# The start of a four-layer trunk: modulation in two halves of the features, the stream scaled in place, plain transposes, the context last

## The chip, the cores and the metric

The kernel is one program on one core of a Trainium2 chip. The metric is the device time in microseconds, the median of several runs. PE is TensorE, DVE VectorE, ACT ScalarE, POOL GpSimd and SP SyncE, which issues the DMAs.

## What is computed

Four layers (two HGRN2 recurrences, two short convolutions, each followed by a SwiGLU block) over a latent stream x of 1024 tokens by 1024 features and a context of 256 tokens, in fp32. The part at issue is the entry of the first layer:

```python
silu_c = jax.nn.silu(c)
silu_cc = jax.nn.silu(c_ctx)
...
mod = silu_c @ ada_w[l] + ada_b[l]
sh1, sc1, g1, sh2, sc2, g2 = [m[:, None, :] for m in jnp.split(mod, N_MOD, axis=-1)]
h = _modulate(_rmsnorm(x, norm_w[l, 0]), sh1, sc1)
...
hc = _modulate(_rmsnorm(ctx, norm_w[l, 0]), csh1, csc1)
```

`_rmsnorm` divides a row by its root mean square and multiplies by norm_w, `_modulate` is h * (1 + scale) + shift. h and hc are then multiplied by w_hgrn_in (1024 x 5120).

## The kernel before

All large products are made of three fp32r passes (`products`, L1396 to L1404): high part by high, low by high, high by low. The features lie on the partitions in the products, so x (tokens on partitions) is turned first. The weights come in panels of 128 output columns; the first two (forget gates of head 0) are split into high and low by GpSimd (`split_to`, L1204 and L1207), the third (`first_third`) by ScalarE and GpSimd.

Each engine has its own list of instructions, written by hand in the order in which they run; semaphores hold them together. What is done at the start:

- **SP** issues the small tables, then 16 blocks of ada_w in four groups of 2 MB (`ada_group`; groups 0 and 1 make the shift of features 0 to 511 and 512 to 1023, groups 2 and 3 the scale), panel 0, half of x, panel 1, the context, the other half of x.
- **Modulation.** Groups 0 and 2 are summed by VectorE (`start_acc`, 16 instructions each, L2809 and L2813; PE then adds over the partitions with ones, `start_sums`, L1541). Groups 1 and 3 are products of PE with the conditions padded to 128 columns (`start_products`, 8 products each, L1521); ScalarE copies the row out of PSUM (`ada_turn`) and PE turns it (`start_turn`, L1531). Then VectorE adds the bias and weighs (L2707, L2826) into `mods` and `in_scale`.
- **Norms.** ScalarE squares and sums a block of 128 tokens and takes the root (`x_norm`, `x_std`), VectorE the reciprocal, and a diagonal matrix of it (`diag_start`) is made. PE turns a square of x by multiplying with the diagonal (`turn`, L1436): transposed and scaled in one. In a later layer `turn` uses a plain transpose of rows scaled beforehand (L1435).
- **A turn** t covers two blocks of tokens and two of features, four squares. ScalarE modulates even t, VectorE odd t (`modulate`, L2840) into a ring of four tiles `mod_start`; ScalarE rounds to the high part (`h_hi`), VectorE subtracts for the low part (`low`, `h_lo`, L2707) and counts `h_ready`.
- **first_pair** on PE makes both gates' panels: for each half of the tokens and each of eight kb (a step of six products) it waits for `h_ready`, and the turns still to be made are put between the steps. The context's turns (t = 8 to 11) and its two blocks (`context_block`, 24 products of 256 columns each, both into one bank) stand between the two halves. The list goes on with the third panel (`first_third`), and from there on without turns.

An fp32 product (the modulation's, a diagonal's) is recorded as two matmul passes, so 8 products are x16 in the profile; a plain transpose is one.

## Time and profile before

| | |
|---|---|
| median of 3 runs | 2605.58 us (2605.37 to 2605.85) |
| profiled execution, span | 2600.0 us (no time of its own is listed beside the span) |
| PE busy | 2524.9 us, 97% |
| DVE busy | 1750.5 us, 67% |
| POOL busy | 1245.5 us, 48% |
| ACT busy | 1122.8 us, 43% |
| mean granted TensorE clock | 0.991 |
| DMA | 351.05 MB, mean 135 GB/s |

The span goes from the first to the last instruction; busy is the time in which an engine had an instruction, so that two engines' shares overlap. Idle time of an engine that nothing waits for costs nothing. The granted clock is 1 at 2.4 GHz and 0.5 at 1.2 GHz.

### The profile page before, as it was taken

What the parts mean: (1) busy time and instruction counts of PE and PEld (TensorE: products, weight loads), DVE (VectorE), ACT (ScalarE), POOL (GpSimd) and SP (SyncE); (2) the same over time, 40 slices, a digit from 0 to 9 for tenths busy, and PEclk for the clock granted to TensorE, in tenths of its full rate; (3) what the DMA queues carried; (4) which work ended last, traced back from release to release, by engine and by line L of the source; (5) the groups of instructions that cost most, each with busy time, mean ns of one, the idle gap of its engine ahead of it and who ended that gap; (6) DMA issues with size and microseconds to landing.
All of it is one profiled execution on the core that took longest, in us unless ns stands there. A gap on an engine that the chain in (4) does not pass through costs nothing.

```text
span 2600.0 us, 35820 instructions
## 1 busy us (share of the span) xinstructions
PE 2524.9 (97%) x12452; PEld 2115.7 (81%) x12452; DVE 1750.5 (67%) x2343; ACT 1122.8 (43%) x2124; POOL 1245.5 (48%) x811
## 2 busy tenths in 40 slices
PE   7999999999999989999999999999999999999998
PEld 5888888888878778888888877888787888888886
DVE  5377777767865566667667986666436555565888
ACT  5334534443443653343445475111264333434444
POOL 3121321432230037776768952444304776766983
PEclk8999999999999999999999999999999999999999
DMA  6223431441361343343456332333514323345533
GB/s 261 74 74 121 178 136 67 154 146 65 114 264 61 138 141 130 122 145 129 165 204 238 97 110 97 115 112 113 214 54 154 106 89 109 116 166 216 191 99 114
DMA packets 119634, 351.05 MB, mean 135 GB/s; under 512 B 12240, under 2 KB 12240, under 8 KB 116432
## 3 DMA queue, kind: packets, MB, share of 16 engines
q1 hardware_dynamic: 119504, 349.33, 38.1%
q8 instruction: 80, 1.31, 0.2%
q14 instruction: 50, 0.41, 0.0%
HBM read 258.58 MB, written 90.70 MB: 134 GB/s over the span
## 4 chain that ended last, share of the span: by engine, by line
PE 83%; DVE 7%; POOL 3%; ACT 3%; DMA 2%; issue 1%; SPq 1%; DVEq 0%; ACTq 0%; POOLq 0%
PE psum L1402 19%; PE psum L1403 19%; PE psum L1404 19%; PE psum L1975 4%; PE psum L1977 4%; PE psum L1976 4%; PE psum L1650 2%; PE psum L1652 2%; PE psum L1651 2%; PE psum L1602 2%; POOL row_unit_sum L1358 2%; PE psum L1616 1%; PE psum L1589 1%; PE psum L1572 1%; DVE k_all L2999 1%
## 5 line engine op out<-in xcount | busy, mean ns | idle before, releaser
L1402 PE MATMUL psum<-x_hi,unit 128*128 128x512 f32 x1232 | 481.5, 391 | 5.2 <-DVE x_lo L2707 5.2
L1403 PE MATMUL psum<-x_lo,unit 128*128 128x512 f32 x1232 | 480.0, 390 | 0.0
L1404 PE MATMUL psum<-x_hi,unit 128*128 128x512 f32 x1232 | 479.9, 390 | 0.0
L2707 DVE TENSOR_TENSOR c_set<-c_set,psum 128x512 f32<-128x512 f32 x352 | 233.8, 685 | 279.3 <-ACT c_set L2072 178.6
L1308 POOL TENSOR_TENSOR unit<-unit_sum,unit 128x512 fp32r<-128x512 f32 x200 | 294.4, 1480 | 5.8 <-ACT unit L2072 4.9
L1402 PEld LDWEIGHTS psum<-x_hi,unit 128*128 128x128 f32 x1232 | 231.9, 188 | 54.2 <-ACT c_set L2072 5.7
L1404 PEld LDWEIGHTS psum<-x_hi,unit 128*128 128x128 f32 x1232 | 231.7, 188 | 48.5
L1403 PEld LDWEIGHTS psum<-x_lo,unit 128*128 128x128 f32 x1232 | 231.9, 188 | 47.6
L1402 PE MATMUL psum<-h_hi,w_hi 128*128 128x512 f32 x624 | 262.6, 421 | 0.2 <-DVE h_lo L2707 0.2
L1975 PE MATMUL psum<-row_unit_hi,part_hi 128*128 128x512 f32 x616 | 241.8, 392 | 3.1 <-DVE part_lo L2707 1.8
L1404 PE MATMUL psum<-h_hi,w_lo 128*128 128x512 f32 x624 | 244.1, 391 | 0.0
L1403 PE MATMUL psum<-h_lo,w_hi 128*128 128x512 f32 x624 | 243.9, 391 | 0.0
L1977 PE MATMUL psum<-row_unit_hi,part_lo 128*128 128x512 f32 x616 | 240.5, 390 | 0.0
L1976 PE MATMUL psum<-row_unit_lo,part_hi 128*128 128x512 f32 x616 | 240.3, 390 | 0.0
L2707 DVE TENSOR_TENSOR part_lo<-part_raw,part_hi 128x512 fp32r<-128x512 f32 x154 | 186.1, 1211 | 64.0 <-ACT part_hi L2072 63.5
L2072 ACT ACTIVATE c_set<-psum 128x512 f32<-128x512 f32 x176 | 100.3, 597 | 265.3 <-PE psum L1404 265.3
L1302 POOL TENSOR_TENSOR unit_sum<-ffn_raw 128x512 f32<-128x512 f32 x80 | 108.6, 1357 | 197.2 <-PE psum L1402 197.2
L1302 POOL TENSOR_TENSOR unit_sum<-ffn_raw,ffn_raw 128x512 f32<-128x512 f32 x120 | 159.8, 1332 | 58.5 <-PE psum L1402 58.0
L1222 POOL TENSOR_TENSOR w_lo<-w_raw,w_hi 128x1024 fp32r<-128x1024 f32 x30 | 73.5, 2449 | 238.6 <-ACT w_hi L2072 238.6
L2072 ACT ACTIVATE unit<-unit_sum 128x512 fp32r<-128x512 f32 x200 | 126.0, 630 | 55.8 <-POOL unit_sum L1302 55.8
L1975 PEld LDWEIGHTS psum<-row_unit_hi,part_hi 128*128 128x128 f32 x616 | 116.1, 188 | 29.4 <-issue 3.4
L1402 PE MATMUL psum<-conv_h_hi,conv_w_hi 128*128 128x512 f32 x352 | 138.1, 392 | 0.4 <-POOL conv_w_lo L1207 0.4
(320 smaller groups left out, 5630.9 us busy)
## 6 DMA issues: line engine op xcount, KB each, us to landing
ffn_raw<-in_w_ffn_in SPq DMA_DIRECT2D x80, 512.0 KB, 5.1
part_raw<-parts_kept SPq DMA_DIRECT2D x154, 256.0 KB, 2.7
parts_kept<-part_sums SPq DMA_DIRECT2D x22, 1280.0 KB, 5.3
out_raw<-in_w_ffn_out SPq DMA_DIRECT2D x44, 512.0 KB, 7.4
w_raw<-in_w_hgrn_in SPq DMA_DIRECT2D x40, 512.0 KB, 3.6
ada_raw<-in_ada SPq DMA_DIRECT2D x32, 512.0 KB, 4.8
conv_ada_raw<-in_ada SPq DMA_DIRECT2D x32, 512.0 KB, 4.1
units_kept<-stage_unit SPq DMA_DIRECT2D x28, 512.0 KB, 2.9
```

What stands on the lines that cost most here:

```text
L1222: pool.tensor_tensor(place[1][:, :], w_raws[0][:, slot, :], place[0][:, :], ALU.subtract).then_inc(S["panel_split"], 1)
L1302: pool.tensor_tensor(units[(PRODUCTS * e + l) % 4][2][:, :], one, other, op).then_inc(S["unit_summed"], 1)
L1308: pool.tensor_tensor(unit[1][:, :], unit[2][:, :], unit[0][:, :], ALU.subtract).then_inc(S["unit_ready"], 1)
L1358: pool.tensor_tensor(row_unit(n)[2][:, :], one, other, op).then_inc(S["rows_summed"], 1)
L1402: begin = pe.matmul(out_ap, hi[:, a:b], rhs_hi, start=first, stop=False)
L1403: pe.matmul(out_ap, hi[:, a:b], rhs_lo, start=False, stop=False)
L1404: return begin, pe.matmul(out_ap, lo[:, a:b], rhs_hi, start=False, stop=last)
L1975: begin = pe.matmul(dst, of_hi[:, tokens], hi[:, :], start=g == 0, stop=False)
L1976: pe.matmul(dst, of_hi[:, tokens], lo[:, :], start=False, stop=False)
L1977: return begin, pe.matmul(dst, of_lo[:, tokens], hi[:, :], start=False, stop=g == FFN_GROUPS - 1)
L2072: nc.scalar.activation(dst, src, func, **kw).then_inc(S[sem], 1)
L2707: V.tensor_tensor(dst, a, b, op).then_inc(S[sem], 1)
```

## The change

SP loads panel 0 first, then groups 2 and 0 (scale and shift of features 0 to 511), the small tables, panel 1, half of x, groups 3 and 1, the rest of x, and the context at the end. The modulation is made in two halves. In each half the scale is 8 products of PE, and the shift is shared: VectorE sums the first half of its rows (8 instructions), PE multiplies the other (4 products), and PE adds both in one accumulation. VectorE copies three of the four rows out of PSUM. x and the context are scaled by VectorE in place (128 x 1024 for a block), `diag_start` is dropped, and `turn` becomes a plain transpose for this layer too. PE makes 22 idle products at the start instead of 12. The second half's modulation stands behind the first step of `first_pair`; the context's turns, norms and blocks come last. ScalarE loads the root's table ahead of the first block.

```diff
+START_ROWS = 2, 0, 3, 1
...
-SCALED = 2, 3
+SCALED = 0, 2, 3
...
-TURNS = ([(q, f) for f in range(4) for q in (0, 1)] + [(CTX_Q, f) for f in range(4)]
-         + [(q, f) for f in range(4) for q in (2, 3)],
+TURNS = ([(q, f) for f in range(4) for q in (0, 1)] + [(q, f) for f in range(4) for q in (2, 3)]
+         + [(CTX_Q, f) for f in range(4)],
          None,
...
-NORMED = ((0, 1, 2, 3, 8, 9, 4, 5, 6, 7), tuple(range(LAT)))
+NORMED = (tuple(range(LAT + CCH)), tuple(range(LAT)))
...
         def diag_of(inst, block):
-            i = normed(inst).index(block)
-            return diag_start[:, i % 6, :] if inst == 0 else diag[:, i % 4, :]
+            return diag[:, normed(inst).index(block) % 4, :]
 
         def scaled_of(inst, block):
 
+            if inst == 0:
+                return stream(0, block)
             return ys[0][block // 4][:, block % 4, :] if inst == 2 else x_scaled[block % 3][:, :]
...
-            small_load(cond_in[:, :], cond)
+            sp.dma_start(cond_in[:, :], cond).then_inc(S["cond_loaded"], 16)
...
+            panel(N_HEADS, 0, w_hgrn_in[0])
+            ada_group(START_ROWS[0])
+            ada_group(START_ROWS[1])
             small_load(bias[:, :], ada_bias)
             small_load(nw[:, :], norm_w)
             small_load(lbr[:, :], lb_raw)
             small_load(gn[:, :], gnorm)
             small_load(cw[:, :], conv_w)
...
-            for group in range(4):
-                ada_group(group)
-            panel(N_HEADS, 0, w_hgrn_in[0])
+            panel(N_HEADS + 1, 1, w_hgrn_in[1])
             x_load(x_start, 0)
             x_load(x_start, 1)
-            panel(N_HEADS + 1, 1, w_hgrn_in[1])
-            sp.dma_start(ctxt[:, :, :], ctx.rearrange("b p n -> p b n")).then_inc(S["ctx_loaded"], 16)
+            ada_group(START_ROWS[2])
+            ada_group(START_ROWS[3])
             x_load(x_start, 2)
             x_load(x_start, 3)
+            sp.dma_start(ctxt[:, :, :], ctx.rearrange("b p n -> p b n")).then_inc(S["ctx_loaded"], 16)
...
             def start_products(i):
 
-                g = 2 * i + 1
+                g = START_ROWS[i]
+                if i == 3:
+                    pe.wait_ge(S["ada_row_evac"], i)
                 pe.wait_ge(S[f"ada_first{g}"], 16)
-                for kb in range(KB):
+                first = 0 if g >= 2 else KB // 2
+                for kb in range(first, KB):
                     mm = pe.matmul(ada_row_out[i], cond_pad[:, kb, :],
                                    ada_first[:, ADA_GROUP * g + kb // 2, (kb % 2) * HALF:(kb % 2 + 1) * HALF],
-                                   start=(kb == 0), stop=(kb == KB - 1))
+                                   start=(kb == first), stop=(kb == KB - 1))
                 mm.then_inc(S["ada_row_full"], 1)
...
             def start_turn(i):
-                g = 2 * i + 1
+
+                g = START_ROWS[i]
                 pe.wait_ge(S["ada_row_evac"], i + 1)
+                if g < 2:
+                    pe.wait_ge(S["start_step"], KB * (g + 1))
                 for j in range(ADA_GROUP):
                     c = 2 * (ADA_GROUP * g + j)
-                    mm = pe.matmul(ada_first_out[:, c:c + 2], ada_turn[:, i, j * P:(j + 1) * P], ident[:, 0:2],
-                                   start=True, stop=True)
+                    mm = pe.matmul(ada_first_out[:, c:c + 2], ada_turn[:, i % 2, j * P:(j + 1) * P], ident[:, 0:2],
+                                   start=True, stop=g >= 2)
+                    if g < 2:
+                        for cond_of in range(2):
+                            mm = pe.matmul(ada_first_out[:, c + cond_of:c + cond_of + 1],
+                                           start_acc[:, g, cond_of, j * P:(j + 1) * P], ones[:, :],
+                                           start=False, stop=cond_of == 1)
                 return mm
...
-            for _ in range(12):
+            for _ in range(22):
                 pe.matmul(bank(2, 0, P), ident[:, :], ident[:, :], start=True, stop=True)
             pe.wait_ge(S["silu_done"], 2)
             start_products(0)
-            start_sums(0)
+            start_products(1)
             start_turn(0)
-            start_products(1)
-            start_sums(1)
             start_turn(1).then_inc(S["ada_first_done"], 1)
-            for t in range(5):
+            for t in range(4):
                 turn(0, t)
+            start_products(2)
...
+                    turns_at = {(0, 5): (8,), (0, 6): (9,), (0, 7): (10,), (1, 0): (11, 12), (1, 1): (13,), (1, 2): (14,),
+                                (1, 3): (15,), (1, 4): (16,), (1, 5): (17,), (1, 6): (18,), (1, 7): (19,)}
...
-                            pe.wait_ge(S["h_ready"], 12 * half + 2 * (kb // 2) + 2)
+                            pe.wait_ge(S["h_ready"], 8 * half + 2 * (kb // 2) + 2)
...
-                            if half == 0 and kb < 7:
-                                turn(0, 5 + kb)
-                            elif half == 1 and kb < 2:
-                                turn(0, 18 + kb)
-                        if half == 0:
-                            for t in range(12, 15):
+                            if (half, kb) == (0, 0):
+                                start_products(3)
+                                start_turn(2)
+                                start_turn(3).then_inc(S["ada_first_done"], 1)
+                                for t in range(4, 8):
+                                    turn(0, t)
+                            for t in turns_at.get((half, kb), ()):
                                 turn(0, t)
-                            pe.wait_ge(S["h_ready"], 12)
-                            context_block(0, 0)
-                            turn(0, 15)
-                            turn(0, 16)
-                            context_block(1, 1)
-                            turn(0, 17)
+                    pe.wait_ge(S["h_ready"], 20)
+                    context_block(0, 0)
+                    context_block(1, 1)
...
+            copy(junk_start[:, 0:1], eps[:, 0:1], "table_ready", ACT.Sqrt)
+            act.wait_ge(S["table_ready"], 1)
+
+            def x_norms(blocks):
+                for tb in blocks:
+                    if tb % 2 == 0:
+                        act.wait_ge(S[f"x_loaded{tb // 2}"], 16)
+                    x_norm(0, tb, junk_start)
+
+            x_norms(range(4))
+            act.wait_ge(S["cmod_done"], 3)
+            for t in range(4):
                 turned(0, t)
-            for tb in range(4, LAT):
-                if tb % 2 == 0:
-                    act.wait_ge(S[f"x_loaded{tb // 2}"], 16)
-                x_norm(0, tb, junk_start)
-            for t in range(8, 12):
+            act.wait_ge(S["ada_row_full"], 3)
+            copy(ada_turn[:, 0, :], ada_row_out[2], "ada_row_evac")
+            x_norms(range(4, LAT))
+            act.wait_ge(S["cmod_done"], 7)
+            for t in range(4, 8):
                 turned(0, t)
...
+                for t in range(8, 12):
+                    turned(0, t)
+                act.wait_ge(S["ctx_loaded"], 16)
+                for c in range(CCH):
+                    x_norm(0, LAT + c, junk_start)
                 gates_out(0)
                 for t in range(12, 16):
                     turned(0, t)
-                evacuate_ctx(0, z[FWD][:, 0:CTX])
-                for t in range(16, 18):
-                    turned(0, t)
-                evacuate_ctx(1, z[BWD][:, 0:CTX])
-                for t in range(18, 20):
+                act.wait_ge(S["panel_loaded0"], 32)
+                copy(first_third[0][:, :], w_raws[0][:, 0, :], "w_hi_done")
+                act.wait_ge(S["cmod_done"], 8)
+                for t in range(16, 20):
                     turned(0, t)
                 gates_out(1)
+                evacuate_ctx(0, z[FWD][:, 0:CTX])
+                evacuate_ctx(1, z[BWD][:, 0:CTX])
...
-                if inst in SCALED:
+                if inst in SCALED[1:]:
                     return
                 dve.wait_ge(S["x_rstd_done"], n + 1)
+                if inst == 0:
+                    V.tensor_scalar(stream(0, block), stream(0, block), x_rstd[:, c], None, ALU.mult
+                                    ).then_inc(S["diag_done"], 1)
+                    return
...
+            def start_sums(g):
+
+                dve.wait_ge(S[f"ada_first{g}"], 16)
+                for kb in range(KB // 2):
...
+            def start_row(i):
+
+                dve.wait_ge(S["ada_row_full"], i + 1)
+                if i >= 2:
+                    dve.wait_ge(S["ada_first_done"], 1)
+                V.tensor_copy(ada_turn[:, i % 2, :], ada_row_out[i]).then_inc(S["ada_row_evac"], 1)
...
+            dve.wait_ge(S["silu_done"], 1)
+            start_sums(0)
+            dve.wait_ge(S["small_loaded"], 16 * 5)
+            dve.wait_ge(S["params"], 1)
...
+            start_row(0)
             dve.wait_ge(S["consts"], 5)
-            for tb in range(4):
-                x_norm(0, tb)
-            dve.wait_ge(S["ada_first_done"], 1)
-            sums = ada_first_out.rearrange("p (m two) -> p two m", two=2)
-            tt(mods[:, 0:2 * KB], sums[:, 0, :], bias[:, 0:2 * KB], ALU.add, "cmod_done")
-            tt(cmods[:, :], sums[:, 1, :], bias[:, 0:2 * KB], ALU.add, "cmod_done")
-            dve.wait_ge(S["cmod_done"], 2)
-
-            def weigh(dst, scale, weights, sem):
-
-                V.scalar_tensor_tensor(dst, scale, 1.0, weights, ALU.add, ALU.mult).then_inc(S[sem], 1)
-
-            weigh(in_scale[:, 0:KB], mods[:, KB:2 * KB], nw[:, 0:KB], "cmod_done")
-            weigh(in_scale[:, 4 * KB:5 * KB], cmods[:, KB:2 * KB], nw[:, 0:KB], "cmod_done")
-            dve.wait_ge(S["cmod_done"], 4)
+            x_norm(0, 0)
+            start_row(1)
+            x_norm(0, 1)
+            start_mods(0)
+            x_norm(0, 2)
+            x_norm(0, 3)
...
+            for t in range(4):
+                start_turned(t)
+            low(0, 3)
+            start_sums(1)
+            x_norm(0, 4)
+            x_norm(0, 5)
+            start_row(3)
+            x_norm(0, 6)
+            start_mods(1)
+            modulate(5)
+            low(0, 4)
+            x_norm(0, 7)
+            low(0, 5)
+            for t in range(6, 20):
+                if t % 2 == 1:
+                    modulate(t)
+                if t == 12:
+                    x_norm(0, LAT)
+                    x_norm(0, LAT + 1)
+                if t > 6:
                     low(0, t - 1)
             low(0, 19)
```

### Order of the instructions at three places

Place 1: PE from its first product to the first product of the stream. Before:

```order
L1545 MATMUL psum<-ident 128x128 x12
L1521 MATMUL psum<-ada_first,cond_pad 128x512 x8
L1541 MATMUL psum<-ones,start_acc 128x1 x8
L1531 MATMUL psum<-ident,ada_turn 128x2 x4
L1521 MATMUL psum<-ada_first,cond_pad 128x512 x8
L1541 MATMUL psum<-ones,start_acc 128x1 x8
L1531 MATMUL psum<-ident,ada_turn 128x2 x4
L1436 MATMUL psum<-diag_start,x_start 128x128 x20
L1402 MATMUL psum<-h_hi,w_hi 128x512
```

And now (the rows of the second start turn stand shortened here, then the four turns, the third row's products, the first step's first product, and the fourth row's products behind that step):

```order
L1550 MATMUL psum<-ident 128x128 x22
L1527 MATMUL psum<-ada_first,cond_pad 128x512 x12
L1540 MATMUL psum<-ident,ada_turn 128x2 x5
L1544 MATMUL psum<-ones,start_acc 128x1 x2
...
L1438 MATMUL psum<-ident,x_start 128x128 x16
L1527 MATMUL psum<-ada_first,cond_pad 128x512 x8
L1405 MATMUL psum<-h_hi,w_hi 128x512
...
L1527 MATMUL psum<-ada_first,cond_pad 128x512 x4
```

All modulation stood ahead of the first turn; now half of it stands behind turns 0 to 3, eight of its products directly ahead of the stream's first product.

Place 2: VectorE from the parameters of the forget gates (`lb_exp`, `lb`, `q_scale`) and the sums to its first reciprocals. Before, the parameters stood ahead of all sums:

```order
L2722 RECIPROCAL lb_exp<-lb_exp 128x8
L2707 TENSOR_TENSOR lb_exp<-lb_exp 128x8
L2707 TENSOR_TENSOR lb<-lb_exp 128x8
L2728 TENSOR_SCALAR one_minus_lb<-lb 128x8
L2730 TENSOR_SCALAR q_scale<-one_minus_lb 128x8
L2809 TENSOR_SCALAR start_acc<-ada_first,silu_cond 128x512 x2
L2813 SCALAR_TENSOR_TENSOR start_acc<-ada_first,silu_cond,start_acc 128x512 x14
```

And now, from the first sums to the second row copy:

```order
L2789 SCALAR_TENSOR_TENSOR start_acc<-ada_first,silu_cond,start_acc 128x512 x6
L2700 TENSOR_TENSOR lb_exp<-lbr,lb_exp 128x8
L2829 RECIPROCAL lb_exp<-lb_exp 128x8
L2700 TENSOR_TENSOR lb_exp<-lb_exp 128x8
L2700 TENSOR_TENSOR lb<-lb_exp 128x8
L2835 TENSOR_SCALAR one_minus_lb<-lb 128x8
L2837 TENSOR_SCALAR q_scale<-one_minus_lb 128x8
L2797 COPY ada_turn<-psum 128x512
L2713 RECIPROCAL x_rstd<-x_std 128x1
L2718 TENSOR_SCALAR x_start<-x_start,x_rstd 128x1024
L2797 COPY ada_turn<-psum 128x512
```

The parameter instructions, two row copies and the first scaling have come between the sums and PE's second start turn, which waits for the second row copy.

Place 3: VectorE in the second half of the tokens, around the context's scaling (the first h_lo is the low of turn 10, the second that of turn 11). Now:

```order
L2857 TENSOR_SCALAR mod_start<-psum,in_scale,mods 128x256 x2
L2700 TENSOR_TENSOR h_lo<-mod_start,h_hi 128x2x256
L2713 RECIPROCAL x_rstd<-x_std 128x1
L2718 TENSOR_SCALAR ctxt<-ctxt,x_rstd 128x1024
L2713 RECIPROCAL x_rstd<-x_std 128x1
L2718 TENSOR_SCALAR ctxt<-ctxt,x_rstd 128x1024
L2700 TENSOR_TENSOR h_lo<-mod_start,h_hi 128x2x256
```

Before, four diagonals for blocks 4 to 7 stood at the like place, ahead of the lows of the context's last two turns:

```order
L2840 TENSOR_SCALAR mod_start<-psum,in_scale,cmods 128x256 x2
L2738 RECIPROCAL x_rstd<-x_std 128x1
L2750 TENSOR_SCALAR diag_start<-ident,x_rstd 128x128
...
L2707 TENSOR_TENSOR hc_lo<-mod_start,hc_hi 128x512 x2
```

The low of turn 11, for which the third step of the second half waits, now stands behind both scalings of the context.

## Rows read from the trace of the kernel before

**Rows 1.** Busy time by stretch: us; busy (instructions) of each engine; granted clock; DMA; GB/s
```profile
45.22:91.07 45.85, 42.29 (x264) 37.16 (x265) 27.15 (x51) 27.05 (x53) 2.61 (x1) 1.00 0.13 39
68.30:71.28 2.98, 2.98 (x24) 2.98 (x25) 2.15 (x4) 1.98 (x4) 0.00 (x0) 1.00 0.60 176
91.07:130.00 38.93, 38.93 (x188) 32.87 (x187) 5.17 (x8) 14.17 (x18) 7.18 (x3) 1.00 0.27 94
```

**Rows 2.** Timeline of PE: start us, duration us, engine, line, operation, count
```profile
16.85 8.49 PE L1521 MATMUL psum<-ada_first,cond_pad 128*128 128x512 f32 x16 [9.80 <-DMA ada_first<-in_ada]
...
27.77 7.11 PE L1521 MATMUL psum<-ada_first,cond_pad 128*128 128x512 f32 x16
34.73 1.84 PE L1541 MATMUL psum<-ones,start_acc 128*128 128x1 f32 x16
...
46.68 1.05 PE L1436 MATMUL psum<-diag_start,x_start 128*128 128x128 f32 x8
47.49 0.48 PE L1402 MATMUL psum<-h_hi,w_hi 128*128 128x512 f32 x1
...
91.07 0.39 PE L1402 MATMUL psum<-h_hi,first_third_hi 128*128 128x512 f32 x1
```

**Rows 3.** Chain of waits, start of the program: start us, us, what
```profile
36.01 1.05 ACT junk_start L2072 x2
...
45.22 0.47 PE psum L1402
```

**Rows 4.** Timeline of SP's queue, DMA issues (columns as in rows 2)
```profile
1.27 0.42 SPq L804 DMA_DIRECT2D bias<-in_ada_bias  x1
...
3.63 4.95 SPq L834 DMA_DIRECT2D ada_first<-in_ada  x4
```

**Rows 5.** Timeline of VectorE
```profile
7.91 0.17 DVE L2730 TENSOR_SCALAR q_scale<-one_minus_lb 128x8 f32<-128x8 f32 x1
11.69 0.88 DVE L2809 TENSOR_SCALAR start_acc<-ada_first,silu_cond 128x512 f32<-128x512 f32 x2 [3.61 <-DMA ada_first<-in_ada]
12.49 9.36 DVE L2813 SCALAR_TENSOR_TENSOR start_acc<-ada_first,silu_cond,start_acc 128x512 f32<-128x512 f32 x14
...
39.33 1.17 DVE L2826 SCALAR_TENSOR_TENSOR in_scale<-mods,nw 128x8 f32<-128x8 f32 x1
...
49.54 0.69 DVE L2707 TENSOR_TENSOR h_lo<-mod_start,h_hi 128x512 fp32r<-128x512 f32 x1 [0.18 <-ACT h_hi L2072]
...
64.81 3.44 DVE L2707 TENSOR_TENSOR hc_lo<-mod_start,hc_hi 128x512 fp32r<-128x512 f32 x2
...
128.64 0.83 DVE L3053 TENSOR_SCALAR gates_f<-gates_f 128x1280 f32<-128x1280 f32 x1
```

**Rows 6.** Timeline of GpSimd
```profile
28.31 5.45 POOL L1204 TENSOR_TENSOR w_hi<-w_raw,zero 128x1024 fp32r<-128x1024 f32 x1 [19.12 <-DMA w_raw<-in_w_hgrn_in]
...
36.16 1.88 POOL L1204 TENSOR_TENSOR w_hi<-w_raw,zero 128x1024 fp32r<-128x1024 f32 x1
38.12 2.35 POOL L1207 TENSOR_TENSOR w_lo<-w_raw,w_hi 128x1024 fp32r<-128x1024 f32 x1
65.09 2.61 POOL L1222 TENSOR_TENSOR first_third_lo<-w_raw,first_third_hi 128x1024 fp32r<-128x1024 f32 x1 [24.62 <-ACT first_third_hi L2072]
```

**Rows 7.** Busy time by stretch, PE alone: us, PE busy, granted clock
```profile
7.05:9.42 2.37, 0.00 (x0) 1.00 1.00 410
9.42:19.66 10.24, 2.81 (x4) 0.50 1.02 414
40.14:43.54 3.40, 3.40 (x19) 0.50 1.02 405
```

**Rows 8.** Timeline of PE, plain transposes in a later stage
```profile
1879.73 0.60 PE L1435 MATMUL psum<-ident,x_scaled 128*128 128x128 f32 x4
1880.08 0.48 PE L1650 MATMUL psum<-conv_row,mixed_hi 128*128 128x512 f32 x1
```

**Rows 9.** Timeline of ScalarE
```profile
74.03 0.36 ACT L2072 ACTIVATE z_f<-psum 128x256 f32<-128x256 f32 x1
```

128 lines of the change are left out of this document (47 added, 81 removed).

## The prediction

> **What bounds the kernel now.** Read the busy time by stretch first [rows 1]: from 91.07 to 130 us PE is busy without a gap, and between 45.22 and 91.07 us it is idle for 3.6 of 45.85 us. At 91.07 us stands the third panel's first product [rows 2]; from there on the program is the same in both kernels, so what moves this start moves the end by as much, and I carry the rest over unchanged. The chain of waits [rows 3] names the first GEMM product at 45.22 us as the end of the start-up. The sum is made against the span of the profiled execution, 2600.0 us; the median of the runs, 2605.58 us, is 5.6 us above it and I add the difference in time to the median. A measurement of this kernel can tell about 0.2%, 5.2 us, from no change.
>
> **When the data land.** The first large transfer was issued at 3.63 us and its 2 MB were used at 11.69 us; the next group at 16.85 us, so a group takes 5.16 us and the rest, 2.9 us, is latency [rows 2, 4, 5]. After the change the first weight panel (0.5 MB, 1.3 us) goes out at 1.27 us, the second issue's slot, so it lands at about 5.4, ada group 2 at 10.6, group 0 at 15.8. Then the small tables and panel 1 (about 18), the stream's first two parts (20.5 and 23), groups 3 and 1 (28 and 33), the rest by 41 us. None of the later ones is waited for.
>
> **The new front half.** VectorE's sums over group 0 are now 8 instructions: 0.8 us for the first two, 6 x 0.67 us from 9.36 us / 14 [rows 5], 4.8 us in all, from 15.8 to 20.6. PE's 8 products on group 2 cost 7.1 us at full clock (the second x16 of [rows 2]) and end at about 17.7, the 4 on group 0 end at 21.3. They are not on the path of VectorE. On VectorE stand next the five parameter instructions (0.2 us each [rows 5], and a wait for ScalarE's exponential: 1.2 us), a row copy from PSUM (0.6), a block's scaling in place, another row copy (0.6). The scaling in place is 128x1024 and not in the trace; below it stands the 128x1280 tensor_scalar at 0.83 us, so 0.7 us, plus 0.2 for the reciprocal: 0.9 (bounds 0.8 and 1.4). Sum: 20.6 + 3.3 = 23.9 us.
>
> To this comes **GpSimd**. It splits panel 1 with two instructions of 1.88 and 2.35 us, and panel 1 now lands during VectorE's sums. In the trace such an instruction and VectorE's never ran at the same time: GpSimd's first took 5.45 us while the sums ran, against 1.88 alone [rows 6], and VectorE's 128x8 weighing took 1.17 us and its pair of lows 3.44 us instead of 1.3 while GpSimd was in one [rows 5]. At the first gap, behind the first parameter instruction, GpSimd gets in, and again behind the third. I take the full 1.88 + 2.35 = 4.2 us (bounds 0 and 4.2), so the second row copy ends at 28.1 us.
>
> The Trainium skill, SBUF — State Buffer, section SBUF: two separate sides, says that the pair of ports goes to whichever of the two engines starts first, for the whole instruction. The rows agree on the blocking, but not on who is next: GpSimd waited through five of VectorE's instructions from 28.31 us on, and through one behind 64.81 us [rows 5, 6]. By the page alone my sum, 2609.0 us, stands; the first of these two rows makes room for the second rival.
>
> Then PE turns the second row and adds the sums: 4 + 8 small products, 24 passes at 1.84/16 = 0.115 us, 2.7 us: 30.8. Modulation of the first half 0.7, two more blocks scaled 1.8: 33.3. Turns 1 to 3 at 0.4 us: 34.5. Here PE meets start_products(2), 8 products, 7.1 us: 41.6. First GEMM step 1.4 us (six products; 1.46 from 45.22 to 46.68 with the start of the first [rows 2, 3]): 43.0. **So the first GEMM product comes at about 41.6 instead of 45.2, but alone.** Behind it stand 4 more products (3.6), the two turns (0.9 and 2.7): 50.2. And PE is idle from 21.3 to about 26.5, so its clock falls: in the trace idling from 7.1 us brought the granted clock to half (1.2 GHz) at 9.42 us, where it stayed until 19.66, after 2.8 us of dense products; and the small products from 34.7 us on, with turns and a pause behind them, brought it down again at 40.14 for 3.4 us [rows 2, 7]. I charge one such stretch at half speed under the products, 3.4 / 2 = 1.7 us (bounds 0 and 6). The last start turn ends at **51.9 us**.
>
> **From there to the third panel.** PE has 16 turns, 15 GEMM steps and the two context blocks. A turn by a diagonal took 0.81 us from 46.68 to 47.49 [rows 2], and about 0.08 more in the product behind it; four plain transposes of the same size took 0.35 from 1879.73 to 1880.08 [rows 8], so 0.44 with the same extra. 16 x 0.44 + 15 x 1.38 + 5.9 (two context blocks, 2.98 us each [rows 1]) = 33.7 us. The saving of transposes, 20 x 0.45 = 9 us, is what the change truly removes; the 8 added products (7.1 us) give most of it back. Four waits remain. From a turn's end to the product that uses it I count 2.85 us for modulate, high and low: the turn whose last pass went out by 47.49 [rows 2] had its second low done at 50.23 [rows 5], and 0.1 for the handover.
> - Turn 9 stands in front of only one GEMM step and a turn: 2.85 - 1.8 = 1.0 us.
> - Turn 11 stands behind the first step of half 1. ScalarE does its high part and then the context's two norms (2 x 1.37 us: 1.05 for the squares [rows 3], the rest the root and handovers), and VectorE's low of turn 11 stands behind both scalings of the context (the third place of the order shown above). So 2.0 + 2.7 + 0.9 + 0.8 = 6.4 us after the turn, with 2.2 us of cover: 4.2 us.
> - Turn 19 is the last thing before context_block(0, 0), with no cover: 2.85 us.
> - Both context blocks use one bank; the copy of 0.36 us [rows 9] and its two handovers: 0.8 us.
>
> Together 8.9 us, where before it lost 3.6 [rows 1]. 51.9 + 33.7 + 8.9 = **94.5 us** against 91.07: 3.4 us later, 2609.0 us.
>
> **Costed at nothing:** the 22 idle products (they end near 9.1 us, before the data at 10.6; without them the products on group 2 would start at half clock and end some 1.5 us later, while the second row's copy waits for VectorE until 27.5 in any case); ScalarE's early table load (at about 21 us, ahead of the second block); the small tables behind group 0 (the parameters wait for group 0 anyway); the dropped diagonals; ScalarE's copy of the third panel's first part, now behind turned(15) (needed some 15 us later). The modulation's shift by PE and VectorE together saves VectorE 16 instructions of 0.67 us; the half of it that goes from the path is in the 4.8 us above.
>
> **The rivals.**
> 1. *PE at half clock longer* (slower). The small start products at 27 to 31 us and at 47 to 51 us keep PE sparse, as those at 34.7 us did. If the clock is at 1.2 GHz in start_turn(1), in all of the first 7 us of products and again in the first GEMM steps, that adds 2 + 1.7 + 1.7: 96 to 100 us, 2611 to 2615 us. For: the pause on PE ahead of them, over 5 us, is longer than the 2.4 us after which the clock fell the first time, and the second fall came with PE three quarters busy. Against: it was back 2.8 us after dense products began at 16.85 us. It decides when the products of start_products(2) still run at half after the first 3 us.
> 2. *GpSimd is kept out* until VectorE waits for PE at 28 us: the 4.2 us fall away, 2604.8 us. For: five instructions passed it at 28.31 us. Against: the parameter chain has gaps, and GpSimd's pass of 65.09 us was let in behind the one VectorE instruction that was running.
> 3. *The front half pays off* (faster): no collision, clock kept, and the context's norms finding ScalarE early, so that the 4.2 us wait halves: 94.5 - 4.2 - 1.7 - 2.1 = 86.5, 2601.0 us, and a little less in each price gives over 0.2%. For: PE has 9 us less of transposes. Against: it needs all three.
> 4. *It does not do what it says:* the first product no earlier than 45 us, as start_products(2) stands ahead of it. That is a half of rival 1, not a case of its own.
>
> **Chances.** Forecast 0.38, rival 1 0.34, rival 2 0.16, rival 3 0.12. The forecast and rival 2 lie within 0.2% (0.54); rival 1 is slower (0.34), rival 3 faster (0.12). The range reaches from the middle of rival 3 to the end of rival 1, 2601 to 2615 us.
>
> **What would show it.** First GEMM product near 42 to 45 us; a pause of 4 us on PE in half 1 before its third step, ended by VectorE; another near 3 us before the context products; GpSimd's w_hi of panel 1 longer than 4 us, or parameter instructions of VectorE of 2 us; granted clock 0.5 between 24 and 35 us; third panel at 94 us. I would be wrong if PE passes from the start turns to 90 us with under 5 us idle, or if anything behind the third panel has moved.

## The result, and the profile after

The changed kernel took 2613.49 us (median of 5 runs, 2612.66 to 2615.98), the kernel before 2605.37 us (5 runs, 2604.80 to 2605.85). The ratio is 1.0036, 95% interval 1.0025 to 1.0048: 8.1 us slower, more than the 0.2% that a measurement can tell from no change. The forecast was 2609.0 us, and its likeliest case "within 0.2%"; what came lies in rival 1's 2611 to 2615 us, and so inside the range.

Busy time by stretch of the changed kernel, from the first GEMM product to the third panel (columns as in rows 1), and behind it the three stretches at half clock up to there (columns as in rows 7):

```profile
47.68:101.99 54.31, 46.65 (x250) 38.53 (x249) 29.62 (x58) 29.80 (x57) 2.40 (x1) 0.94 0.09 28
```

PE alone:

```profile
25.60:42.70 17.10, 13.65 (x52) 0.50 1.03 409
56.40:59.80 3.40, 3.40 (x18) 0.51 0.00 0
80.20:83.70 3.50, 3.50 (x11) 0.51 0.00 0
```

Against [rows 1] the stretch grew from 45.85 to 54.31 us: PE is idle there for 7.66 us instead of 3.56, and busy for 4.36 us more although it turns by plain transposes; but the stretch now also holds the fourth row's products and two start turns (7.3 us, from 49.47 to 56.73), and the clock is 0.94 instead of 1. Ahead of it, half speed lasts from 25.6 to 42.7 us, where before it fell mostly into an idle wait for data [rows 7]. The timeline of PE (columns as in rows 2):

```profile
26.30 1.87 PE L1540 MATMUL psum<-ident,ada_turn 128*128 128x2 f32 x8 [5.19 <-DVE ada_turn L2797]
29.33 0.58 PE L1540 MATMUL psum<-ident,ada_turn 128*128 128x2 f32 x2 [1.17 <-DVE ada_turn L2797]
...
34.47 1.09 PE L1438 MATMUL psum<-ident,x_start 128*128 128x128 f32 x4
37.15 2.80 PE L1438 MATMUL psum<-ident,x_start 128*128 128x128 f32 x12 [1.58 <-DVE x_start L2718]
39.74 8.51 PE L1527 MATMUL psum<-ada_first,cond_pad 128*128 128x512 f32 x16
47.68 0.79 PE L1405 MATMUL psum<-h_hi,w_hi 128*128 128x512 f32 x1
...
56.73 3.42 PE L1438 MATMUL psum<-ident,x_start 128*128 128x128 f32 x16
59.90 0.48 PE L1405 MATMUL psum<-h_hi,w_hi 128*128 128x512 f32 x1
...
71.80 0.50 PE L1405 MATMUL psum<-h_hi,w_hi 128*128 128x512 f32 x1 [0.73 <-DVE h_lo L2700]
...
80.04 0.64 PE L1405 MATMUL psum<-h_hi,w_hi 128*128 128x512 f32 x1 [3.89 <-DVE h_lo L2700]
...
95.42 0.39 PE L1405 MATMUL psum<-hc_hi,w_hi 128*128 128x256 f32 x1 [2.56 <-DVE hc_lo L2700]
...
99.03 0.38 PE L1405 MATMUL psum<-hc_hi,w_hi 128*128 128x256 f32 x1 [0.47 <-ACT z_f L2076]
...
101.99 0.40 PE L1405 MATMUL psum<-h_hi,first_third_hi 128*128 128x512 f32 x1
```

The first GEMM product stands at 47.68 us, 2.5 us later than before [rows 2]; I had expected it 3.6 us earlier. The third panel stands at 101.99 us instead of 91.07, 10.9 us later. start_turn(1) goes from 29.33 to 34.47 us: 5.1 us for 24 passes, 0.21 us for each where [rows 2] show 0.115. The four waits of the second part (0.73, 3.89, 2.56, 0.47 us) are 7.65 us.

What PE waited for until 26.30 and 29.33 us are two row copies of VectorE, and these stand behind its sums. Three of the six longer sums, from windows of VectorE's timeline that hold one each:

```profile
17.83 0.75 DVE L2789 SCALAR_TENSOR_TENSOR start_acc<-ada_first,silu_cond,start_acc 128x512 f32<-128x512 f32 x1
18.49 2.38 DVE L2789 SCALAR_TENSOR_TENSOR start_acc<-ada_first,silu_cond,start_acc 128x512 f32<-128x512 f32 x1
20.80 2.82 DVE L2789 SCALAR_TENSOR_TENSOR start_acc<-ada_first,silu_cond,start_acc 128x512 f32<-128x512 f32 x1
```

What follows them on VectorE:

```profile
24.64 0.20 DVE L2829 RECIPROCAL lb_exp<-lb_exp 128x8 f32<-128x8 f32 x1 [0.27 <-ACT lb_exp L2076]
...
25.56 0.68 DVE L2797 COPY ada_turn<-psum 128x512 f32<-128x512 f32 x1
27.73 0.16 DVE L2713 RECIPROCAL x_rstd<-x_std 128x1 f32<-128x1 f32 x1 [1.49 <-ACT x_std L2076]
27.93 0.75 DVE L2718 TENSOR_SCALAR x_start<-x_start,x_rstd 128x1024 f32<-128x1024 f32 x1
28.59 0.68 DVE L2797 COPY ada_turn<-psum 128x512 f32<-128x512 f32 x1
```

And in the timeline of its ScalarE:

```profile
24.39 0.21 ACT L2076 ACTIVATE lb_exp<-lb_exp 128x8 f32<-128x8 f32 x1 [6.19 <-DVE lb_exp L2700]
24.62 1.28 ACT L2076 ACT_TABLE_LOAD   x1
...
26.15 1.06 ACT L2076 ACTIVATE junk_start<-x_start 128x1024 f32<-128x1024 f32 x1
```

The 8 sums of VectorE end at 24.2 us, not 20.6. The third of the six took 0.75 us, the fourth 2.38 and the fifth 2.82, and beside these two stand the two passes of GpSimd over panel 1:

```profile
17.98 2.35 POOL L1207 TENSOR_TENSOR w_hi<-w_raw,zero 128x1024 fp32r<-128x1024 f32 x1 [4.57 <-DMA w_raw<-in_w_hgrn_in]
20.41 2.67 POOL L1210 TENSOR_TENSOR w_lo<-w_raw,w_hi 128x1024 fp32r<-128x1024 f32 x1
```

The high pass ended at 20.33 us and the fourth sum 0.55 us behind it; the low pass ended at 23.08 and the fifth sum again 0.55 us behind it. So each pass held up one sum, and both together cost 3.7 us (7.78 us for the six sums, where e2 below has 4.06).

Then ScalarE: it sat 6.19 us in front of the exponential that waits for VectorE's parameter, loaded the root's table, and only at 26.15 us began the norm of a block that had been there since about 20.5 us. So VectorE waited 1.49 us, and the second row copy stands behind that wait.

### The profile page after: what moved, and what is told of

Its sections match the earlier page's. It is cut to its first block, busy times and chain, and to the rows that moved or that the text cites. A ratio compares the mean times of both kernels' runs of the same rounds, so it can differ in the third digit from the quotient of the medians.

```text
span 2613.1 us, 35752 instructions
## 1 busy us (share of the span) xinstructions
PE 2537.0 (97%) x12424; PEld 2121.4 (81%) x12424; DVE 1748.5 (67%) x2338; ACT 1121.3 (43%) x2120; POOL 1242.3 (48%) x811
## 4 chain that ended last, share of the span: by engine, by line
PE 85%; DVE 6%; POOL 3%; ACT 2%; issue 2%; DMA 2%; SPq 0%; DVEq 0%; ACTq 0%; POOLq 0%
PE psum L1405 19%; PE psum L1407 19%; PE psum L1406 19%; PE psum L1979 4%; PE psum L1981 4%; PE psum L1980 4%; PE psum L1654 2%; PE psum L1656 2%; PE psum L1655 2%; PE psum L1606 2%; POOL row_unit_sum L1361 2%; PE psum L1620 1%; PE psum L1593 1%; PE psum L1576 1%; PE psum L1438 1%
## 5 line engine op out<-in xcount | busy, mean ns | idle before, releaser
L1979 PEld LDWEIGHTS psum<-row_unit_hi,part_hi 128*128 128x128 f32 x616 | 115.6, 188 | 29.3 <-issue 3.4
L1407 PEld LDWEIGHTS psum<-h_hi,w_lo 128*128 128x128 f32 x624 | 117.4, 188 | 25.7
```

Source lines behind the costliest of these rows:

```text
L1407: return begin, pe.matmul(out_ap, lo[:, a:b], rhs_hi, start=False, stop=last)
L1979: begin = pe.matmul(dst, of_hi[:, tokens], hi[:, :], start=g == 0, stop=False)
```

## The experiments

Twelve kernels were run, four or two at a time on one chip together with the kernel before. The medians of before in these sets were 2603.39 to 2604.37 us, with single runs from 2601.7 to 2609.0, so single edits are told apart better by where the third panel starts in the trace than by the time. Each position is read from the one profiled execution of its kernel. Half clock is the sum of the stretches at 0.5 up to the third panel.

| kernel | ratio to before, 95% | third panel, us | first GEMM product | half clock, us |
|---|---|---|---|---|
| before | | 91.07 | 45.22 | 13.7 |
| changed | 1.0036 (1.0025 to 1.0048) | 101.99 | 47.68 | 23.9 |
| e1, PE kept busy | 1.0033 (1.0022 to 1.0044) | 99.96 | 45.59 | 13.7 |
| e2, split of panel 1 late | 1.0022 (1.0012 to 1.0031) | 98.20 | 43.84 | 20.5 |
| e3, tables first | 1.0028 (1.0019 to 1.0037) | 102.24 | 44.92 | 27.3 |
| e4, context late | 1.0019 (1.0010 to 1.0028) | 98.04 | 47.73 | 20.5 |
| e5, row copies together | 1.0036 (1.0024 to 1.0048) | 100.40 | 46.08 | 23.9 |
| e6, before with plain transposes | 1.0010 (1.0001 to 1.0019) | 93.49 | 47.86 | 27.3 |
| e7, four edits | 0.9999 (0.9990 to 1.0009) | 93.16 | 39.75 | 20.5 |
| e8, 12 idle products | 1.0046 (1.0033 to 1.0060) | 102.37 | 46.43 | 30.7 |
| e9, e7 with turns early | 0.9981 (0.9972 to 0.9990) | 87.20 | 40.18 | 17.1 |
| e10, e9 with dense passes | 0.9981 (0.9972 to 0.9990) | 87.17 | 40.61 | 13.7 |
| e11, e9 filled | 0.9978 (0.9969 to 0.9987) | 88.29 | 40.36 | 13.7 |
| e12, e11 and start_turn(3) | 0.9988 (0.9979 to 0.9997) | 91.52 | 42.10 | 17.1 |

What lies behind the third panel is not quite the same in each execution: span less third panel was 2508.9 us before, 2511.1 in the changed kernel, and 2507.9 to 2511.5 in the others. The clock is a part of it, not all: of this rest 36.1 us were at half clock before and 43.2 us in the changed kernel, but 40.0 us in e1, which has the longest rest, and 31.9 us in e12, whose rest is 2510.4 us.

### e1: is it the pauses that cost the clock?

```diff
             start_products(1)
+            idle_products(20)
             start_turn(0)
+            idle_products(4)
             start_turn(1).then_inc(S["ada_first_done"], 1)
-            for t in range(4):
+            turn(0, 0)
+            idle_products(9)
+            for t in range(1, 4):
                 turn(0, t)
```

> Edit: idle products on PE (20 ahead of start_turn(0), 4 ahead of start_turn(1), 9 between the first and the second turn), so that PE is not idle while it waits for VectorE. Clock theory: in the changed kernel start_turn(1) took 5.1 us where full clock gives 2.7, turns 1 to 3 took 2.6 instead of 1.2 and start_products(2) 8.5 instead of 7.1; with PE kept busy the granted clock stays at 1 from 21 to 48 us, the first GEMM product comes at about 44 us instead of 48.1, turns 4 to 7 take 1.8 us, and the third panel starts near 96.5 us instead of 102.2: 5 to 6 us faster, about 2608 us. Rival, the chain of VectorE and GpSimd: turns 1 to 3 wait for the scalings of blocks 2 and 3 anyway, so at most 2.4 us of the 5 come through, about 2611 us. If the idle products push out the products on which the program waits, no gain at all.

Measured: third panel 2.0 us earlier, and no difference in time that can be shown. From 10.6 us up to the first GEMM product PE had no pause over 1 us, and the clock fell all the same, 5.1 us later than in the changed kernel, inside start_turn(1). Busy time by stretch of e1, PE alone:

```profile
30.70:37.50 6.80, 6.80 (x34) 0.50 1.03 410
```

PE's timeline in e1, and VectorE's:

```profile
34.23 3.74 PE L1534 MATMUL psum<-ident 128*128 128x128 f32 x18
37.81 1.47 PE L1438 MATMUL psum<-ident,x_start 128*128 128x128 f32 x12
```

```profile
35.12 0.75 DVE L2726 TENSOR_SCALAR x_start<-x_start,x_rstd 128x1024 f32<-128x1024 f32 x1
```

Ten us less at half clock gave 2.0 us. That is the rival's size, but not by its cause alone. Up to 29.3 us PE waits for VectorE in both kernels, so that the clock gives nothing there. Behind it the steps got 3.9 us shorter: start_turn(1) 1.1 us (3.98 instead of 5.14), turns 1 to 3 1.3 us, start_products(2) 1.5 us. About 1.8 us of this went to the nine idle products, which ran at half clock themselves and took 3.7 us: VectorE's scaling of block 3 ended at 35.87 us, and turn 1 had to wait behind them until 37.81.

### e2: GpSimd out of the sums

```diff
-            for slot in range(2):
-                split_to(N_HEADS + slot, slot, ring[slot])
+            split_to(N_HEADS, 0, ring[0])
+            pool.wait_ge(S["ada_row_evac"], 2)
+            split_to(N_HEADS + 1, 1, ring[1])
```

> Edit: GpSimd starts splitting panel 1 only when both row copies of VectorE are done (ada_row_evac at 2). Collision theory: VectorE's sums then end at about 21 us instead of 24.2 (its hole of 2.6 us from 20.95 on goes) and the split, 4.2 us, falls into 28 to 33 us, where VectorE waits for PE; the second row copy ends 1.5 to 3.5 us earlier, and the third panel with it: about 2611 us. Rival: ScalarE's norm of block 0 (exponential behind VectorE, table load, x) is the later one, so that the row copy gains nothing and the split now meets the modulation instead: no change or 1 us slower.

The third panel came 3.8 us earlier, a little more than the theory had for the row copy (1.5 to 3.5); 0.25 us of it is an earlier landing of group 0. VectorE's six last sums took 4.06 us where they had taken 7.78, and GpSimd met a scaling of VectorE that nothing waited for (2.42 us instead of 0.75). VectorE's timeline in e2:

```profile
16.26 4.06 DVE L2790 SCALAR_TENSOR_TENSOR start_acc<-ada_first,silu_cond,start_acc 128x512 f32<-128x512 f32 x6
...
25.43 2.42 DVE L2719 TENSOR_SCALAR x_start<-x_start,x_rstd 128x1024 f32<-128x1024 f32 x1
```

So the collision costs 3.7 us, all of it on the path. The rival falls: ScalarE's norm moved forward as well, since its exponential had waited for the same sums.

### e3: the small tables and the parameters first

```diff
             panel(N_HEADS, 0, w_hgrn_in[0])
+            small_load(bias[:, :], ada_bias)
...
+            small_load(cw[:, :], conv_w)
             ada_group(START_ROWS[0])
             ada_group(START_ROWS[1])
-            small_load(bias[:, :], ada_bias)
...
```

On VectorE the parameter block moves ahead of start_sums(0).

> Edit: SP issues the five small tables ahead of both modulation groups, and VectorE does its six parameter instructions before the sums instead of behind them. ScalarE then has its exponential and the root's table before x lands. Theory: the row copy follows the sums at once (1.3 us earlier) and x_norm(0, 0) starts at 20.5 us when x lands instead of 26.2; the second row copy ends about 2.5 us earlier, at 26.8 instead of 29.3 us. Third panel 2 to 3 us earlier, about 2611 us. Rival: group 0 lands later by what the small tables take of the DMA engines, up to 2 us, which gives most of it back: same within 1 us.

Group 0 landed 1.7 us later (first sum at 17.37 instead of 15.71), and the second row copy still ended 1.3 us earlier; with a shorter half clock in front (13.7 us instead of 17.1) the first GEMM product came 2.8 us earlier. But the third panel stood at 102.24: behind that product the clock was low for 13.7 us (53.0 to 59.9, 80.3 to 83.7 and 94.0 to 97.4 us) instead of 6.9. The rival's result, and its cause took a part only: the later landing cost about half of the gain at the row copy, the clock the rest.

### e4: the context out of the way of turn 11

```diff
-                act.wait_ge(S["ctx_loaded"], 16)
-                for c in range(CCH):
-                    x_norm(0, LAT + c, junk_start)
                 gates_out(0)
-                for t in range(12, 16):
+                for t in range(12, 14):
+                    turned(0, t)
+                act.wait_ge(S["ctx_loaded"], 16)
+                for c in range(CCH):
+                    x_norm(0, LAT + c, junk_start)
+                for t in range(14, 16):
                     turned(0, t)
```

VectorE does x_norm(0, LAT) and x_norm(0, LAT + 1) behind low(0, 13) instead of ahead of low(0, 11).

> Edit: ScalarE does the context's two norms behind turned(13) instead of ahead of turned(12), and VectorE scales the context behind low(13) instead of ahead of low(11). Theory: the pause of 3.9 us ahead of the third step of half 1 falls to under 1 us (turn 11 to product is 2.85 us, cover 2.2), and the stretch at half clock behind it (1.7 us) goes too: 3 to 5 us faster, 2608.5 to 2610.5 us. Rival: the same wait turns up later, ahead of the fifth or seventh step (turns 13 to 15) or of the context's turns, since ScalarE has the same 2.7 us of norms and 1.2 us of gates to do: under 1 us faster.

Third panel 4.0 us earlier. The wait of 3.89 us is 0.30, a new one of 0.78 stands ahead of the context's first turn, and the half clock from 80.2 us on is gone. PE's timeline in e4:

```profile
76.52 0.50 PE L1405 MATMUL psum<-h_hi,w_hi 128*128 128x512 f32 x1 [0.30 <-DVE h_lo L2702]
...
82.63 0.63 PE L1438 MATMUL psum<-ident,ctxt 128*128 128x128 f32 x4 [0.78 <-DVE ctxt L2720]
```

### e5: both row copies together

```diff
             start_row(0)
+            start_row(1)
             dve.wait_ge(S["consts"], 5)
             x_norm(0, 0)
-            start_row(1)
             x_norm(0, 1)
```

> Edit: VectorE makes both row copies one behind the other and only then scales blocks 0 and 1. In the changed kernel the second row copy stood behind x_norm(0, 0), which waited 1.5 us for ScalarE's root at 27.6. Theory (the start hangs on the chain of VectorE up to start_turn(1)): the second copy ends at about 26.9 instead of 29.3 us, the modulation and the third panel come about 2.4 us earlier, about 2611 us. Rival (data and ScalarE's norms bound the turns as well): the scalings of blocks 2 and 3 stand in front of turns 1 to 3 in either order, so that under 1 us comes through.

1.6 us came through of the expected 2.4 (third panel 100.40), because start_turn(0), 1.9 us at half clock, now stands in the path ahead of start_turn(1). The clock stretches are as in the changed kernel, 23.9 us.

### e6: one part of the change alone, on the kernel before

```diff
-SCALED = 2, 3
+SCALED = 0, 2, 3
...
+                if inst == 0:
+                    V.tensor_scalar(stream(0, block), stream(0, block), x_rstd[:, c], None, ALU.mult
+                                    ).then_inc(S["diag_done"], 1)
+                    return
```

ScalarE's four diagonals are dropped; loads, sums and order stay.

> The kernel before with one part of the change alone: x and the context are scaled in place by VectorE and turned by plain transposes, ScalarE's four diagonals fall away; loads, modulation and order stay. Theory: the 20 turns cost 0.44 instead of 0.89 us each. 5 of them stand before the first GEMM product (45.22 us) and gain 2 us at most; 15 stand between it and 91.07, where PE was idle for 3.6 us only: 6 to 7 us less work, of which a part turns into waits for modulate, high and low (2.85 us each, as in the changed kernel). Third panel at 84 to 88 us, that is 3 to 7 us faster than before. Rival: the chain of modulate, high and low on VectorE and ScalarE, and VectorE's scalings of 0.75 us in place of the 128x128 diagonals, bound these steps already, so that the time is the same within 1.5 us.

Neither: the third panel came 2.4 us **later**, the time is 1.0010 of before. The first GEMM product is 2.6 us later, and from it to the third panel it takes 45.63 us, as before (45.85). The saving of 0.45 us for each turn is there and is lost to waits. PE's timeline in e6:

```profile
47.86 0.47 PE L1404 MATMUL psum<-h_hi,w_hi 128*128 128x512 f32 x1 [1.37 <-DVE h_lo L2705]
...
66.45 0.89 PE L1437 MATMUL psum<-ident,x_start 128*128 128x128 f32 x4 [2.56 <-DVE x_start L2741]
70.26 1.94 PE L1437 MATMUL psum<-ident,x_start 128*128 128x128 f32 x8 [2.91 <-DVE x_start L2741]
...
78.22 0.39 PE L1404 MATMUL psum<-hc_hi,w_hi 128*128 128x256 f32 x1 [1.67 <-ACT z_f L2074]
```

VectorE's timeline in e6:

```profile
34.05 2.87 DVE L2741 TENSOR_SCALAR x_start<-x_start,x_rstd 128x1024 f32<-128x1024 f32 x1
...
66.46 2.84 DVE L2741 TENSOR_SCALAR x_start<-x_start,x_rstd 128x1024 f32<-128x1024 f32 x1
```

A diagonal took VectorE 0.28 us or was ScalarE's; a block's scaling takes 0.75, and 2.8 us when it meets a GpSimd pass, and each stands in front of a turn that PE waits for. A further 6.8 us at half clock (66.7 to 73.5 us) begin right behind the first of the two long pauses. So the plain transposes did not pay here, where the scaling stood on the path.

### e7: four edits together

The edits of e2, e4 and e5, and in place of e3's a cheaper one: only the table for the exponential (lb_raw) is loaded right behind cond, and VectorE's parameters stand ahead of the sums.

```diff
             sp.dma_start(cond_in[:, :], cond).then_inc(S["cond_loaded"], 16)
+            sp.dma_start(lbr[:, :], lb_raw).then_inc(S["cond_loaded"], 16)
```

> The changed kernel with four edits: GpSimd's split of panel 1 behind both row copies; context norms and scalings late; both row copies together ahead of the scalings; the table of the exponential loaded right behind cond, with VectorE's parameter instructions ahead of the sums. If the gains add up (3.7 for the split, 4.0 for the context, 2.4 for the copies, 1.3 for the parameters) the third panel stands at 90 to 91 us instead of 102 and the time is within 1.5 us of before, 2602 to 2605 us. If start_turn(1) directly behind the products on group 0 also keeps full clock, 2 to 3 us less than that, and it beats before. Rival: the turns of the first blocks come to wait for x (landed at 20.5 and 23 us) and for ScalarE's norms, 1.37 us for each block, so that of the 7.4 us at the front only 4 to 5 come through: 2605 to 2608 us.

Third panel 8.8 us earlier than in the changed kernel (the three edits alone sum up to 3.8 + 4.0 + 1.6 = 9.4), time that of before. The first GEMM product came at 39.75, 5.5 us ahead of before. PE does wait ahead of the first turns (1.50 and 1.18 us), as the rival said, but not for x or its norms: ScalarE began the first norm at 20.13 us, when x had landed, and VectorE had no wait for a norm. GpSimd's two passes now meet the scalings of blocks 0 and 1, and the 1.50 us are for the second of these. VectorE's timeline in e7:

```profile
22.12 2.42 DVE L2721 TENSOR_SCALAR x_start<-x_start,x_rstd 128x1024 f32<-128x1024 f32 x1
...
24.64 2.66 DVE L2721 TENSOR_SCALAR x_start<-x_start,x_rstd 128x1024 f32<-128x1024 f32 x1
```

### e8: 12 idle products instead of 22

```diff
-            for _ in range(22):
+            for _ in range(12):
```

> The changed kernel with 12 idle products at the start, as before, instead of 22. My account costed them at nothing: without them the products on group 2 start at half clock, PE's two start products end up to 1.5 us later than 21.1 us, still before VectorE's first row copy at 25.6: same time within 0.5 us, third panel at 102 us. Rival: the clock is then also lower in what follows, or PE's products on group 0 end behind VectorE's sums: 1 to 3 us slower.

PE's products on groups 2 and 0 ran at half clock from 9.6 to 16.5 us and ended at about 23.9 instead of 21.1, 2.8 us later and not up to 1.5; the row copy came at the same time. Busy time by stretch of e8, PE alone:

```profile
9.60:16.50 6.90, 6.11 (x8) 0.51 1.05 396
```

The third panel is at 102.37 us, 0.4 us later, with the clock low at other places behind the products too (30.7 us in all instead of 23.9; the first GEMM product is 1.3 us earlier). The time, 1.0046, can't be told from 1.0036 since the intervals overlap. My price of nothing holds for the third panel; whether 22 save anything stays open.

### e9: the context and turns 8 to 19 early

```diff
-                    turns_at = {(0, 5): (8,), (0, 6): (9,), (0, 7): (10,), (1, 0): (11, 12), (1, 1): (13,), (1, 2): (14,),
-                                (1, 3): (15,), (1, 4): (16,), (1, 5): (17,), (1, 6): (18,), (1, 7): (19,)}
+                    turns_at = {divmod(t - 6, KB): (t,) for t in range(8, 20)}
...
             x_norms(range(4, LAT))
+            act.wait_ge(S["ctx_loaded"], 16)
+            for c in range(CCH):
+                x_norm(0, LAT + c, junk_start)
             act.wait_ge(S["cmod_done"], 7)
```

> The four edits together, with the context done otherwise: ScalarE's two context norms go into its idle time behind the norms of blocks 4 to 7 (it waited 4.0 us for PE there), VectorE scales the context behind low(4), and the twelve turns 8 to 19 stand one behind each step from the third step of half 0 on, so that two steps (2.8 us) lie between turn 19 and the context's products. Theory (the waits of the second part come from the order alone): of the four edits' pauses of 0.73, 0.30, 0.80 and 2.56 us only about 0.1 remains, and the half-clock stretch behind the 2.56 us pause goes: third panel at 87 to 89 us instead of 93.2, 2 to 4 us earlier than before's 91.07, time 2598 to 2601 us. Rival: ScalarE and VectorE (2.3 us for two turns on ScalarE, and the lows) cannot keep up with one turn in 1.8 us and the same pauses come back inside half 1: 92 to 93 us, same as the four edits.

(VectorE scales the context behind low(5), not low(4).) As the first theory said: third panel at 87.20 us, 2597.55 us (median of 11 runs; before 2604.19 in the same set), ratio 0.9981 with the interval 0.9972 to 0.9990. This kernel beats both. Of the waits 0.32 and 0.47 us are left. Half clock remains in two places, the second one with PE busy all the time. Busy time by stretch of e9, PE alone, the last line from the first GEMM product to the third panel:

```profile
24.70:35.00 10.30, 7.08 (x25) 0.50 1.03 409
48.60:55.50 6.90, 6.90 (x29) 0.51 0.00 1
40.18:87.20 47.02, 46.23 (x250) 0.93 0.21 76
```

PE's timeline in e9:

```profile
57.34 0.63 PE L1439 MATMUL psum<-ident,x_start 128*128 128x128 f32 x4 [0.32 <-DVE mod_start L2858]
...
84.23 0.38 PE L1406 MATMUL psum<-hc_hi,w_hi 128*128 128x256 f32 x1 [0.47 <-ACT z_f L2076]
...
87.20 0.40 PE L1406 MATMUL psum<-h_hi,first_third_hi 128*128 128x512 f32 x1
```

### e10 to e12: dense products among the small ones

```diff
                                            start=False, stop=cond_of == 1)
+                        if i == 1:
+                            pe.matmul(bank(2, 0, P), ident[:, :], ident[:, :], start=True, stop=True)
...
+            idle_products(6)
             turn(0, 0)
+            idle_products(7)
```

e10 has the first piece alone, e11 all three, and in e12 the condition is i in (1, 3).

> The same, and one idle product (128x128, 0.21 us at full clock) behind each of the 8 accumulating passes of start_turn(1) and of none of start_turn(3): 1.7 us of added work. Clock theory: with the four edits the granted clock fell in the middle of start_turn(1) at about 24 us, though PE had had no pause; if it is the small passes that bring it down, dense passes between them keep it at 1 up to the first GEMM product, which saves about 2.5 us in the turns and start_products(2) and costs 1.7: within 1 us of the same time, but with granted clock 1 from 24 to 33 us. Rival: the clock falls with the wait for VectorE at 26 us or of itself; then the added products run at half as well, 3.4 us, and the third panel comes 1 to 3 us later.

(The edit puts one idle product behind each of the four feature blocks: 4 products and 0.9 us, not the 8 and 1.7 us that the text above says.) Same time as e9, clock at half from 25.7 to 35.9 us, 1 us later than in e9. It decides nothing: PE still paused 0.87 and 1.18 us.

> The kernel with the turns early, with idle products in all of the first part: one behind each of the four feature blocks of start_turn(1), 6 ahead of the first turn and 7 ahead of the second, so that PE neither pauses nor sends small passes alone from 10 to 37 us. Clock theory (small passes and pauses together bring it down): granted clock 1 from 20 to 36 us, turns 1 to 3 take 1.2 instead of 2.8 us and start_products(2) 7.1 instead of 8.3: first GEMM product at 37.5 to 38.5 instead of 40.2 us, third panel about 85 us, 1.5 to 2.5 us faster than 2597.6. Rival: it falls all the same near 25 us, with dense products in between, and the time is the same or 1 us longer.

> The same, with one idle product behind each of the four feature blocks of start_turn(3) as well (0.9 us of added work). There PE has no pause ahead and the granted clock still was 0.58 from 48 to 56 us. Clock theory: the stretch at half clock behind the small passes goes, which gives back about 3 us in turns 4 to 7 and the first steps: third panel 2 us earlier than with start_turn(1) filled alone. Rival: the stretch stays and the third panel comes 1 us later.

In e11 PE doesn't pause between 21.4 and 56 us, and the clock fell in start_turn(1) and again in start_turn(3). Busy time by stretch of e11, PE alone, the last line ahead of the second fall:

```profile
23.90:30.70 6.80, 6.80 (x34) 0.50 1.02 407
47.80:54.60 6.80, 6.80 (x33) 0.50 0.01 2
40.36:47.80 7.44, 7.44 (x36) 1.00 0.70 280
```

Full clock was back at 30.7 us, so turns 1 to 3 took 1.3 us and the products of start_products(2) 7.03 instead of 8.30; the first GEMM product came at 40.36, as in e9, since the idle products had taken what the clock gave. e12's second stretch stayed too (50.0 to 56.8), and its third panel stood 3.2 us behind e11's; 1.7 of these were lost ahead of the first GEMM product, where the clock had fallen during the products on groups 2 and 0 as well (12.4 to 15.8 us), in PE's list ahead of the edit: group 2 came later there, and PE had waited 1.95 us for it where e11 has 1.09. So the rivals hold in both: with dense products among the small passes, and with the pauses filled, the clock fell in the same places. Times of e9 to e11 can't be told apart.

## Why the prediction was right or wrong

The time lies in the range; the place of the third panel, 94.5 us forecast and 101.99 found, was 7.5 us too early, and the likeliest case was the wrong one. That the time is inside the range is partly luck: by my own rule the median grows by what the third panel is later, so 101.99 us would give 2605.58 + 10.92 = 2616.5 us, above the 2615; for the panel rival 1 had 96 to 100 us. Of the signs I gave, the two waits in the second part and the half clock from 25.6 us on came; the first GEMM product (47.68 us) and the third panel did not come where I said, and what I had called a sign of being wrong, that something behind the third panel moves, came with 2.2 us. By its steps:

- **When the data land**: right. VectorE's first sum stood at 15.71 (15.8 forecast), panel 1 arrived at 17.98 (18). The parameter instructions behind the sums are six and not five, and took 1.3 us for my 1.2.
- **GpSimd, 4.2 us**: right in size (3.7 by e2), wrong in place. I had it enter at the first gap behind the sums; both passes entered between two sums. The signs I gave for it, a high pass of over 4 us or parameter instructions of 2 us, did not show (2.35 us; 0.15 to 0.20 us). Rival 2 falls.
- **ScalarE's exponential and table load, costed at nothing**: wrong, and a step that failed. The exponential waits for VectorE, which waits for group 0 and for GpSimd, and block 0's norm stands behind it. With the wait of 1.49 us the second row copy ended 1.2 us after my 28.1.
- **The clock, 1.7 us**: this is the term that was mis-sized. At half clock start_turn(1) took 2.5 us more than my 2.7, the turns ahead of start_products(2) 1.4, these products 1.3, turns 4 to 7 1.4, and the steps behind the 3.89 us pause 1.7: 8.3 us where I had charged 1.7, 6.6 more, and above my upper bound of 6. Rival 1 had the mechanism and 5.4 us of it, and I gave it 0.34. My point against it, that the clock came back 2.8 us into dense products, was true again (3.0 us into start_products(2)); but most of the loss was ahead of and behind these products.
- **Saving of the transposes, 9 us**: the price of a turn was right, but in e6, where nothing else changes, none of it arrived. I had counted four waits in the second part, which is why the sum for the changed kernel survived; I had not asked whether VectorE's scalings of 0.75 us, in place of 0.28 us diagonals, are themselves the thing waited for.
- **The four waits, 8.9 us**: right. 7.65 us measured (1.0 and 0.73, 4.2 and 3.89, 2.85 and 2.56, 0.8 and 0.47), and the causes are shown: e4 takes out the second by moving the context alone, e9 nearly all of them.
- **The 22 idle products and the third panel's copy at nothing**: right for the third panel as far as the one trace of e8 shows (0.4 us).

Summed up: 94.5 + 1.2 (row copy) + 6.6 (clock) - 1.25 (waits) + 0.95 (left over, in no term) = 102.0 us. The rest was carried unchanged. It holds within the 3.6 us by which the stretch behind the panel differs between the profiled executions, and with that the 10.9 us at the third panel and the medians agree: the interval of the ratio is 6.5 to 12.5 us.

What is shown: the collision by e2, the context's wait by e4, both row copies by e5, and that these make good the change's loss, by e7. The clock's 8.3 us are read from durations. e1, which shortened half clock by 10 us, bears them out in part: the steps on the path got 3.9 us shorter, of which the idle products left 2.0 us at the third panel. Keeping PE busy did not take the half clock away in any run. What makes the clock fall in start_turn(1) and start_turn(3) without a pause stays open: the small passes are what these places have in common, and no run had the place without them.

## What to carry to other kernels

Moving loads forward moves what they trigger: the earlier panel woke GpSimd in the middle of VectorE's only critical sums, and waiting for a semaphore of VectorE gave 3.8 us back at no price. A cheaper operation on a busy engine (a transpose instead of a product) was worth nothing in e6, where the engine that prepares it was not ahead; look first for the idle time in which that preparation fits, as in e9, where the change's own instructions in another order took 0.9981 of the time of before where the change took 1.0036. Idle products that keep an engine busy are on its path too: in e1 nine of them took back 1.8 of 3.9 us. Price small passes on PE at both clocks, and ask for each what lies on either side.
